# The bias tables of prompt attention: made on GpSimd two pairs ahead instead of on VectorE inside a pair

## The reference

```
dist_c = tq[:, None] - c_end[None, :]
sc = jnp.einsum('btghd,bjgd->bghtj', q, kc).astype(jnp.float32) * scale - sl5 * dist_c.astype(jnp.float32)
pc = masked_softmax(sc, dist_c >= 0)
...
ss = jnp.einsum('btghd,bgtnd->bghtn', q, kg).astype(jnp.float32) * scale - sl5 * dist_s.astype(jnp.float32)
ps = masked_softmax(ss, dist_s >= 0)
...
swin = jnp.einsum('btghd,bsgd->bghts', q, kw).astype(jnp.float32) * scale - sl5 * dist_w.astype(jnp.float32)
...
return g[..., 0:1] * oc + g[..., 1:2] * osel + g[..., 2:3] * ow
```

## Time and profile before

| | us |
|---|---|
| median of 3 runs | 2359.99 |
| lowest and highest | 2357.42 and 2362.51 |
| profiled execution, time | 2354.21 |
| profiled execution, span | 2352.4 |
| TensorE busy in the span | 2250.3 (96%) |
| VectorE busy in the span | 1245.7 (53%) |
| ScalarE busy in the span | 665.0 (28%) |
| GpSimd busy in the span | 261.9 (11%) |

### The profile page before, as it was taken

The page is one execution under the profiler, slowest core; times in us unless marked ns, Lnnn a source line. Parts: engine busy times, 40 slices in busy tenths (PEclk is TensorE's granted clock), DMA queues, the critical chain, the costliest instruction groups (busy, mean ns, idle before and its releaser), DMA issues.

```text
span 2352.4 us, 31138 instructions
## 1 busy us (share of the span) xinstructions
PE 2250.3 (96%) x11261; PEld 1728.1 (73%) x11261; DVE 1245.7 (53%) x3247; ACT 665.0 (28%) x1655; POOL 261.9 (11%) x498
## 2 busy tenths in 40 slices
PE   8998999888898999999999999899999999999998
PEld 7556555666586888888888776567878888888887
DVE  1015887655437767777722342234386767777223
ACT  2004877544322222222100120143232222221002
POOL 1001000000001222222000000030022222220000
PEclk9997999999899999999999999999999999999999
DMA  8208200587331223222222213122222322232222
GB/s 198 62 29 253 55 2 2 144 218 206 85 93 55 72 72 105 75 72 89 73 90 72 72 53 101 37 63 82 82 78 72 103 77 72 83 96 72 72 90 104
DMA packets 205819, 207.62 MB, mean 88 GB/s; under 512 B 40395, under 2 KB 192179, under 8 KB 205411
## 3 DMA queue, kind: packets, MB, share of 16 engines
q1 hardware_dynamic: 201650, 187.87, 27.9%
q0 software_dynamic: 4016, 17.75, 2.3%
HBM read 194.23 MB, written 19.69 MB: 91 GB/s over the span
## 4 chain that ended last, share of the span: by engine, by line
PE 90%; DVE 5%; issue 3%; ACT 2%; SPq 0%; DMA 0%; DVEq 0%; POOL 0%; ACTq 0%; POOLq 0%
PE PS L2421 52%; PE PS L2343 4%; PE PS L1362 3%; PE PS L2390 3%; PE PS L2314 2%; PE PS L1448 2%; PE PS L1401 2%; PE PS L1587 2%; PE PS L625 2%; PE PS L639 2%; PE PS L699 2%; PE PS L2283 1%; PE PS L657 1%; PE PS L687 1%; PE PS L713 1%
## 5 line engine op out<-in xcount | busy, mean ns | idle before, releaser
L2421 PE MATMUL PS<-HT,ring 128*128 128x272 f32 x1536 | 373.6, 393 | 0.0
L2421 PE MATMUL PS<-arena,ring 128*128 128x272 f32 x1392 | 341.8, 392 | 0.0
L2421 PEld LDWEIGHTS PS<-HT,ring 128*128 128x128 f32 x1536 | 292.6, 191 | 60.7
L2421 PEld LDWEIGHTS PS<-arena,ring 128*128 128x128 f32 x1392 | 264.3, 190 | 54.4
L2721 ACT ACTIVATE arena<-arena,CB,CW 128x560 f32<-128x560 f32 x128 | 109.3, 854 | 382.6 <-DVE arena L3033 315.9
L2421 PE MATMUL PS<-arena 128*128 128x272 f32 x768 | 194.8, 397 | 12.7 <-DVE arena L2975 12.7
L2421 PE MATMUL PS<-arena,CONST 128*128 128x272 f32 x768 | 191.7, 392 | 0.0
L3048 DVE SCALAR_TENSOR_TENSOR arena<-arena,CW 128x560 f32<-128x560 f32 x256 | 187.3, 788 | 0.0
L2421 PEld LDWEIGHTS PS<-arena 128*128 128x128 f32 x768 | 147.2, 192 | 43.9 <-issue 13.3
L2421 PEld LDWEIGHTS PS<-arena,CONST 128*128 128x128 f32 x768 | 145.9, 190 | 30.1
L3211 POOL COPY arena<-arena 128x16 f32<-128x16 f32 x128 | 50.9, 397 | 636.7 <-DVE arena L3033 535.8
(11 more groups left out here) (447 smaller groups left out, 3518.2 us busy)
## 6 DMA issues: line engine op xcount, KB each, us to landing
ring<-in_w_ffn_up SPq DMA_DIRECT2D x64, 1024.0 KB, 6.4
ring<-in_w_ffn_down SPq DMA_DIRECT2D x32, 1024.0 KB, 5.0
ring<-in_cache_nsa_kv SPq DMA_DIRECT2D x128, 128.0 KB, 3.8
arena<-in_cache_nsa_kv SPq DMA_DIRECT2D x56, 256.0 KB, 6.6
ring<-in_w_ml_in SPq DMA_DIRECT2D x12, 1024.0 KB, 5.7
arena<-in_cache_nsa_win SPq DMA_DIRECT2D x16, 512.0 KB, 5.2
out_nsa_win_sample<-in_cache_nsa_win POOLq DMA_DIRECT2D x8, 1016.0 KB, 15.4
ring<-in_w_nsa_in SPq DMA_DIRECT2D x6, 1024.0 KB, 5.5
```

Of the source, the lines that this page charges most:

```text
L2421: last = mm(PS[:, bank, 0:HALF], lhs[:, k, :], rhs(k), start=(first and k == 0), stop=(done and k == 3))
```

## The change

`bias_tables` moves from VectorE's program to GpSimd's, as the same four scalings per pair. Sets 0 and 1 are made behind the window stores, after a wait for the constants (`s_wg`), and ahead of the wait for the gates. Sets 2 to 7 stand behind the eight window copies, each behind a wait on `s_tt` that is met when pair n-2 no longer needs its set. The wait of the first `biased` of a pair on `s_stg` is as before.

```diff
@@ VectorE, nsa_dve
-            slopes = const("slopes")
             fc = chain
-
-            def bias_tables(n):
-                for g2 in range(2):
-                    sl = slopes[:, 2 * n + g2:2 * n + g2 + 1]
-                    v.tensor_scalar(B2[:, n % 2, g2, :], const("negd"), sl, None, ALU.mult)
-                    last = v.tensor_scalar(BC[:, n % 2, g2].rearrange("p i j -> p (i j)"), const("negc"), sl, None,
-                                           ALU.mult)
-                last.then_inc(s_stg, 1)
...
-            bias_tables(0)
             for p in range(NP + 1):
...
-                if p % 12 == 6 and p // 12 < 7:
-                    bias_tables(p // 12 + 1)
@@ GpSimd
+            slopes = const("slopes")
+
+            def bias_tables(n):
+
+                if n >= 2:
+                    pool.wait_ge(s_tt, 24 * (n - 1))
+                for g2 in range(2):
+                    sl = slopes[:, 2 * n + g2:2 * n + g2 + 1]
+                    g.tensor_scalar(B2[:, n % 2, g2, :], const("negd"), sl, None, ALU.mult)
+                    last = g.tensor_scalar(BC[:, n % 2, g2].rearrange("p i j -> p (i j)"), const("negc"), sl, None,
+                                           ALU.mult)
+                last.then_inc(s_stg, 1)
+
+            pool.wait_ge(s_wg, 32)
+            bias_tables(0)
+            bias_tables(1)
             pool.wait_ge(s_ge, 5)
...
             for b in range(NB):
                 pool.dma_start(wso[b, 0:WIN - NS, :], wsi[b, NS:WIN, :]).then_inc(s_kvo, 16)
+            for n in range(2, 8):
+                bias_tables(n)
```

## The result

The changed kernel takes 2366.79 us (median of 20 runs, 2347.69 to 2375.83); before, measured beside it, takes 2356.04 (20 runs, 2347.10 to 2362.51). The ratio is 1.0045 with a 95% interval of 1.0023 to 1.0066: slower by 0.45%, clear of no change. The profiled execution took 2363.04 us, with a span of 2361.3.

The account below looks back on a forecast made before the run. In prompt attention TensorE and VectorE are both nearly full, and a saved VectorE microsecond counts only where TensorE waits for it. Terms -0.9 + 0 + 0 + 4.5 = +3.6 us on 2359.99 gave 2363.6 us, range 2356 to 2371.

Parts of the forecast that it names:

- signs of being wrong: Border pairs still at 24.0 us, a pair growing by over 1 us, or gate gathers or window copies ending after 416 us.
- Part 1: Start of prompt attention: the first table leaves VectorE's path, so the first biased add comes earlier; 0.9 us gained.
- Part 2: Middle of later pairs: the other seven tables leave VectorE, but TensorE's own queue hides them; gain 0.
- Part 3: GpSimd's queue before attention: two table sets delay the gate copy by 0 to 1.4 us, all hidden; cost 0.
- Part 4: Six borders between pairs: GpSimd's scalings hold VectorE's products; 0.75 us each, a loss of 4.5 us.
- D: Delay on VectorE at each border from GpSimd's scalings; 0.65 to 1.6 us, taken as 0.95.
- The streaming share of 0.44 us: At a border, the part of a 512-column scaling that streams holds VectorE for 0.44 to 0.87 us.
- The 0.2 us of slack: At a border, the first product is ready at 263.83, TensorE takes it at 264.03; subtracted from the delay.
- Sum: Whole kernel: -0.9 + 0 + 0 + 4.5 = +3.6 us, 2363.6 us, counted as the same.
- the clock as a rival: Extra TensorE idle time at borders slows two or three more pairs, 1.7 us each; +7 to +9 us, 2368; chance 0.08.
- The whole-instruction rival: At six borders GpSimd holds VectorE for whole instructions; +5.1 to +11.1 us, 2365 to 2371, middle 2368; chance 0.27.

Follow-up runs that it names:

- e1_first: Against the kernel before, only the tables of pair 0 are made on GpSimd, the other seven stay on VectorE; 2354.82 us against 2355.37, ratio 0.9994.
- e2_left_out: The changed kernel with the tables of pairs 2 to 7 left out; these pairs use the slopes of pairs 0 and 1; 2356.22 us, ratio 0.9995.
- e7_delay: e4_moved with a 400-column memset on VectorE, about 0.4 us, ahead of the border products of pairs 0 to 5; 2366.88 us, ratio 1.0038.
- e4_moved: The changed kernel with GpSimd's release of each later table set 14 biased adds later, away from the border; 2352.34 us, ratio 0.9988.
- e8_moved_again: e4_moved unchanged, measured a second time; 2354.57 us against 2359.24 before, ratio 0.9994.
- e3_dup: The kernel before, all tables on VectorE, while GpSimd makes the six sets of pairs 2 to 7 again into scratch; 2362.95 us, ratio 1.0025.
- e11_after_heads: The changed kernel with VectorE's copy of the finished heads moved two turns later in a pair; 2345.67 us, ratio 0.9954.

## Why the prediction came out as it did

The range (2356 to 2371) held the time, and the likeliest case, no measurable change at +3.6 us, did not happen: the change is slower. That the range held is luck in part. The before measured beside the change is 4 us faster than the one I started from, so the difference is not +6.8 but +10.8 us, the upper end of what the range allowed, and that end had been set for another mechanism. One of the prediction's own signs of being wrong also came: pairs grew by more than 1 us, to 27.4. Point by point:

- **Part 1, 0.9 us gained.** Right in place, a little large in the profile: the first biased add moved from 1.36 to 0.84 us behind the first scores, 0.5 us. I had taken the scores to be ready after 0.41 us, by a later row; VectorE had to wait for them until 0.78 us behind their start (214.26 to 215.04). By the runs, e1_first gained 1.2 (0.3) us at the same clock.
- **Part 2, nothing gained.** Right, and shown: e2_left_out, without any of these tables, is no faster than e1_first, which has them.
- **Part 3, hidden.** Right in the result, wrong in the size. A 512-column scaling takes 1.58 us, above my upper bound of 1.06, and one of 124 columns 0.66, above 0.4. The gate copy starts at 188.48, 4.9 us later instead of 0 to 1.4, and the window copies at 197.16. Nothing waits for them before 416 us, when they have long landed (the copies take 15.5 us from issue, the median). Taking the two-input multiply as an upper bound for a one-input scaling was the error.
- **Part 4, the hold.** Right in mechanism and place, mis-sized: D is 0.40 us, not 0.95, and the price 0.37 us a border, not 0.75. Only the first of four instructions holds anything. One row was misread: the 16-column copy of 0.20 us at 739.89 does not run beside a VectorE instruction that reads PSUM, it starts 0.06 us behind its end. That PSUM-reading adds are not held is shown only by the profile after. The streaming share of 0.44 us that I gave as the lower bound for 512 columns was the value. The 0.2 us of slack did not help: TensorE waits 0.24 us at the border, but the pair is 0.4 us longer, the whole of D.
- **Sum.** -1.3 + 2.2 = +0.9 us at the same clock, where I had +3.6. The 2.2 is itself the difference of two runs; e7_delay against e4_moved and e8_moved_again gives 2.1 for the same delay without GpSimd.
- **The step that failed** is the clock as a rival at 0.08. It carries +10 (2) of the 11 us, and my sum had nothing for it. I had priced one fall at 1.7 us (it is 1.5), and against it I argued that pairs at full clock have their idle stretches already. They have, but that was no protection: those stretches are where the clock falls, and a delay elsewhere in the pair made falls there more frequent. The direct price alone would have been within my 0.2%.
- **The whole-instruction rival** (0.27) gave the right total, 2368, for the wrong reason. The Trainium skill ("SBUF — State Buffer", Who interferes with whom) says that whoever is first gets the shared ports for the whole instruction. The trace agrees that whoever is first wins: GpSimd was ahead by 0.02 us at the borders, and in e3_dup VectorE's first product was ahead by 0.05 and kept its length. It does not bear out the whole instruction: VectorE is held for 0.40 of 1.62 us.

What stays open: why a delay of 0.4 us at the border makes the clock fall more often behind an idle stretch half a pair away. e7_delay and e11_after_heads show that it takes both, the delay and the long stretch; what the chip looks at was not measured. Nor was it tried what GpSimd's reading alone does to VectorE, or what the moved copy does in the kernel before.

## What to carry to other kernels

Work moved to GpSimd can hold VectorE instructions that read and write SBUF only, as the products here: place its release where the next such instructions have slack, or cut it into short instructions. Removing VectorE work that is hidden behind TensorE gave nothing in itself. Moving other VectorE work, the copy of the heads, out from in front of a TensorE wait and into that place gave 0.4 to 0.5%; whether the place had to be emptied first was not tried. Where the granted clock differs from run to run, compare at the same clock too, and look at TensorE's idle stretches even when the direct cost of a change is small.

## What the runs showed of the hardware

- A scaling by a per-partition value takes GpSimd 1.56 us for 512 columns and 0.60 us for 128 (medians), so 2.5 ns a column and 0.28 us fixed; VectorE's spacing for the same 512 columns was 0.4 us.
- A GpSimd scaling holds VectorE's SBUF-to-SBUF product (0.40 us for 512 columns, 0.08 for 128) and then lets it pass while its own instruction goes on for 1.62 us in all; if it starts 0.05 us behind a product, it holds the next one, for 0.30 us. A memset of 512 columns, 0.52 us long, holds for 0.20. Biased adds, which read PSUM, are not held.
- A delay of 0.4 us in six places, worth 2.1 to 2.2 us, came with 8 to 10 us of lower clock (error 2), whether GpSimd or VectorE made it; holds of 0.2 to 0.3 us came with 4.5 to 5.4.
- The same delay with the idle stretch of 1.15 us cut to 0.55 came with no lower clock than before (e11_after_heads, clock part -6.8).
